# x tiles turned in 32x32 blocks by VectorE, straight into the buffer where they are modulated

## The reference, cut to what matters

```python
def rms_norm(x, g):
    y = xf * lax.rsqrt(jnp.mean(xf * xf, axis=-1, keepdims=True) + EPS)
    return (y * g)
...
    h = rms_norm(x, norm_g) * (1 + scale) + shift
    proj = h @ w_in
```

## Time and profile before

| what | us |
|---|---|
| median of 3 runs (1575.09 to 1575.93) | 1575.82 |
| the profiled execution, its own time | 1577.34 |
| its span in the trace | 1575.4 |
| TensorE busy | 1543.2 (98%) |
| VectorE busy | 793.8 (50%) |
| ScalarE busy | 554.5 (35%) |
| GpSimd busy | 824.7 (52%) |

### The profile page before, as it was taken

The page is one execution under the profiler, slowest core; times in us unless marked ns, Lnnn a source line. Parts: engine busy times, 40 slices in busy tenths (PEclk is TensorE's granted clock), DMA queues, the critical chain, the costliest instruction groups (busy, mean ns, idle before and its releaser), DMA issues.

```text
span 1575.4 us, 31999 instructions
## 1 busy us (share of the span) xinstructions
PE 1543.2 (98%) x13128; PEld 1251.8 (79%) x13128; DVE 793.8 (50%) x1946; ACT 554.5 (35%) x1131; POOL 824.7 (52%) x1080
## 2 busy tenths in 40 slices
PE   5999999999999999999999999999999999999998
PEld 2777788877888778888779877888888977888886
DVE  3677455233468875332344775622355775623132
ACT  4334423434332542333432452244433343243330
POOL 2425424457673553455766372437777363437671
PEclk9899999999999999999999999999999999999999
DMA  9732312344565331233265331224465331223351
GB/s 320 224 84 80 84 54 56 107 122 121 174 176 131 92 93 56 68 110 115 85 187 135 88 108 47 77 68 120 147 185 136 88 108 56 70 67 94 106 161 64
DMA packets 304969, 175.83 MB, mean 112 GB/s; under 512 B 74158, under 2 KB 290567, under 8 KB 304808
## 3 DMA queue, kind: packets, MB, share of 16 engines
q1 hardware_dynamic: 304824, 173.79, 38.4%
HBM read 159.69 MB, written 11.96 MB: 109 GB/s over the span
## 4 chain that ended last, share of the span: by engine, by line
PE 93%; DVE 3%; SPq 2%; DMA 1%; issue 1%; ACT 0%; DVEq 0%
PE ps_D L766 55%; PE ps_D L763 24%; SPq L518 2%; PE ps_XD L826 2%; PE ps_XA L924 1%; PE ps_XB L902 1%; PE ps_XA L955 1%; PE ps_XB L950 1%; PE ps_XB L949 1%; DMA th_t<-in_w_ada 1%; PE ps_XA L902 1%; PE ps_XA L935 1%; PE ps_XC L837 0%; PE ps_XC L942 0%; PE ps_XB L935 0%
## 5 line engine op out<-in xcount | busy, mean ns | idle before, releaser
L1698 POOL TENSOR_TENSOR w_lo_t<-w_raw,w_hi_t 128x256 fp32r<-128x256 f32 x928 | 679.9, 766 | 611.9 <-ACT w_hi_t L981 611.6
L766 PE MATMUL ps_D<-h_hi_t,w_hi_t 128*128 128x512 f32 x1024 | 412.2, 403 | 0.0
L766 PE MATMUL ps_D<-h_hi_t,w_lo_t 128*128 128x512 f32 x1024 | 400.2, 391 | 0.0
L766 PE MATMUL ps_D<-h_lo_t,w_hi_t 128*128 128x512 f32 x1024 | 399.9, 391 | 0.0
L981 ACT ACTIVATE w_hi_t<-w_raw 128x1024 fp32r<-128x1024 f32 x232 | 240.6, 1051 | 83.9 <-DMA w_raw<-in_w_out 35.0
L766 PEld LDWEIGHTS ps_D<-h_hi_t,w_hi_t 128*128 128x128 f32 x1024 | 192.4, 188 | 47.2 <-issue 10.0
L766 PEld LDWEIGHTS ps_D<-h_hi_t,w_lo_t 128*128 128x128 f32 x1024 | 192.2, 188 | 41.6
L766 PEld LDWEIGHTS ps_D<-h_lo_t,w_hi_t 128*128 128x128 f32 x1024 | 192.7, 188 | 36.4
L763 PE MATMUL ps_D<-w_hi_t,h_hi_t 128*128 128x384 f32 (+1 forms) x384 | 141.7, 369 | 1.0 <-DVE yf_t L1338 1.0
L763 PE MATMUL ps_D<-w_hi_t,h_lo_t 128*128 128x384 f32 (+1 forms) x384 | 136.6, 356 | 0.0
L763 PE MATMUL ps_D<-w_lo_t,h_hi_t 128*128 128x384 f32 (+1 forms) x384 | 136.6, 356 | 0.0
(11 more groups left out here) (391 smaller groups left out, 2376.2 us busy)
## 6 DMA issues: line engine op xcount, KB each, us to landing
w_raw<-in_w_in SPq DMA_DIRECT2D x72, 512.0 KB, 4.1
w_raw<-in_w_merge SPq DMA_DIRECT2D x64, 512.0 KB, 3.9
w_raw<-in_w_in SPq DMA_DIRECT2D x64, 256.0 KB, 4.0
w_raw<-in_w_out SPq DMA_DIRECT2D x32, 512.0 KB, 4.2
x_or_AT<-in_x_prompt SPq DMA_DIRECT2D x20, 512.0 KB, 5.1
w_raw<-in_w_proj_a SPq DMA_DIRECT2D x64, 128.0 KB, 2.9
w_raw<-in_w_proj_b SPq DMA_DIRECT2D x32, 256.0 KB, 3.2
xr<-in_x_prompt SPq DMA_DIRECT2D x16, 512.0 KB, 5.5
```

What stands on the lines that cost most here:

```text
L766: ins = mm(bank[:, :], w[:, s0, k0 + k, :], a[:, k, :], start=go, stop=end)
L1698: ins = g_.tensor_tensor(w_lo[:, c, k:k + 2], w_raw[:, n % NRAW, k:k + 2], f32(w_hi[:, c, k:k + 2]), ALU.subtract)
```

## The change

The tiles of passes 1 to 3 come from a second copy of x in DRAM, made on the host (outside the timed program), in which each 32x32 block of a tile is placed so that a blockwise transpose gives the turned tile. A row of such a tile holds, in four groups of 256 columns, pieces of four tokens. So the squares are summed per group (four instructions per tile, 16 columns), a new side task `xs` at unit 50 adds and spreads the parts over the partitions by four small matmuls with `eye32` into XC, and VectorE makes 16 scales from it (`group_scales` in place of `row_scales`). ScalarE scales each tile in four parts. VectorE turns the tile by one transpose of 1024 columns from `x_t` into `hf` (`turn_x`, counted by `x_turned`) and modulates in place (`x_mod`). The turn on TensorE and its use of XA and XB are gone for these tiles. SyncE's loads of tiles 2 and 3 wait for `x_turned`.

```diff
-        put(it, 50, 1, "rstd", 0)
+        put(it, 50, 0, "xs", 0, "XC")
...
-            put(it, (60, 61, 63, 64)[_t], 1, "xT", _t, "XB" if _t % 2 else "XA")
+            put(it, (60, 61, 63, 64)[_t], 1, "xT", _t)
...
-                load(x_t[:, t % 2], x[(it + 1) * TB + P * t:(it + 1) * TB + P * t + P, :], f"x_in{t % 2}")
+                load(x_t[:, t % 2], A["x_blocks"][NT * (it + 1) + t], f"x_in{t % 2}")
...
-                    s.wait_ge("xst", 8 + 8 * it + 4)
+                    s.wait_ge("xst", 8 + 16 * it + 8)
                     x_tile(it, 0), x_tile(it, 1)
                 elif what == "x23":
-                    s.full(it, "xT", a - 2)
+                    s.wait_ge("x_turned", NT * it + a - 1)
                     x_tile(it, a)
...
-                if task == "xT":
-                    x_turn(it, a, x_t[:, a % 2])
-                    return
...
+                elif task == "xs":
+                    s.wait_ge("xst", 8 + 16 * (it + 1))
+                    for g in range(4):
+                        ins = mm(bank[32 * g:32 * g + 32, 0:16], eye32[:, :], xst4, start=True, stop=True)
...
             def scale_x(it, t, src):
                 s.wait_ge("rstd", it + 2)
-                s.done(fn(src, src, ACT.Copy, scale=rst[:, t:t + 1]), "xn")
+                if it < 0:
+                    s.done(fn(src, src, ACT.Copy, scale=rst[:, t:t + 1]), "xn")
+                    return
+                for i in range(4):
+                    part = src[:, 256 * i:256 * i + 256]
+                    ins = fn(part, part, ACT.Copy, scale=rst4[:, 4 * t + i:4 * t + i + 1])
+                s.done(ins, "xn")
+
+            def group_squares(src, t, junk):
+                for i in range(4):
+                    s.wait_ge("xst", s.n.get("xst", 0))
+                    s.done(fn(junk, src[:, 256 * i:256 * i + 256], ACT.Square,
+                              accum_out=xst4[:, 4 * t + i:4 * t + i + 1]), "xst")
...
-                s.freed(it, "xT", t)
+                s.wait_ge("x_mod", NT * it + t + 1)
                 s.done(fn(h_hi[:, :, P * t:P * t + P], hf[t % 2], ACT.Copy), "h_hi")
...
+            def group_scales(it, key):
+                s.full(*key)
+                a, t, u = oss, ow1, ow2
+                free(ts(a, bank_of(key)[:, 0:16], 1.0 / D, EPS, ALU.mult, ALU.add), *key)
+                rsqrt(rst4, a, t, u)
+                do(ts(rst4, rst4, 1.0, None, ALU.mult), "rstd")
...
+            def turn_x(it, t):
+                s.wait_ge("xn", NT * (it + 1) + t + 1)
+                s.wait_ge("h_lo", h_tiles(it, t - 2) if t >= 2 else h_tiles(it - 1, t + 2))
+                do(v.transpose(hf[t % 2].rearrange("p k (a q) -> p a k q", a=4),
+                               x_t[:, t % 2].rearrange("p (a k f) -> p a k f", a=4, k=KT)), "x_turned")
+
             def modulate(it, t):
-                s.full(it, "xT", t)
-                s.wait_ge("h_lo", h_tiles(it, t - 2) if t >= 2 else h_tiles(it - 1, t + 2))
-                bank = pb[BANK[(it, "xT", t)]]
                 for k in range(KT):
-                    ins = ts(hf[t % 2][:, k, :], bank[:, P * k:P * k + P], gscale[:, k, 8:9], shift[:, k, 8:9],
+                    ins = ts(hf[t % 2][:, k, :], hf[t % 2][:, k, :], gscale[:, k, 8:9], shift[:, k, 8:9],
                              ALU.mult, ALU.add)
-                free(ins, it, "xT", t)
+                do(ins, "x_mod")
...
-                elif task == "rstd":
-                    row_scales(it)
+                elif task == "xs":
+                    group_scales(it, key)
                 elif task == "xT":
+                    turn_x(it, a)
                     modulate(it, a)
...
-                                    s.full(it - 1, "xT", 3)
-                                    s.freed(it - 1, "xT", 3)
+                                    s.wait_ge("x_mod", NT * it)
...
+def x_blocks(x):
+    return np.ascontiguousarray(x[0].reshape(SEQ // P, 4, 32, KT, 4, 32).transpose(0, 4, 2, 1, 3, 5)).reshape(SEQ // P, P, D)
```

More of the change, by code:

```diff
@@ L255 @@
         + [f"w_in{n}" for n in range(NRAW)] + ["w_hi", "w_lo", "burst", "th_full", "kk", "sq", "ssq", "qa", "k_sc",
-           "lvl", "dgp", "at0", "smax", "p_exp", "p_norm", "kst", "on", "yf", "yh", "yl", "y7f", "y7h", "y7l", "x_in0", "x_in1", "xst", "rstd",
+           "lvl", "dgp", "at0", "smax", "p_exp", "p_norm", "kst", "on", "yf", "yh", "yl", "y7f", "y7h", "y7l", "x_in0", "x_in1", "xst", "rstd", "x_turned", "x_mod",
            "xn", "h_hi", "h_lo", "grow", "s_rows", "s_th", "s_sq8", "s_sc", "s_exp", "s_p", "ckv", "s_oT",
@@ L420, in build @@
         esel = sb("esel", [P, NS], F32R)
-        sm = sb("sm", [P, 688])
+        sm = sb("sm", [P, 720])
         def small(n, start=[0]):
@@ L432, in build @@
         xst, rst, xw1, xw2, xw3 = small(8), small(4), small(4), small(4), small(4)
+        xst4, rst4 = small(16), small(16)
         bst, mv, rs8, t8, u8 = small(12).rearrange("p (a b) -> p a b", a=2), small(2), small(1), small(1), small(1)
@@ L1142, in side @@
                     s.unit_left(it, "pb", 1)
-                    squares(x_t[:, a % 2], a, R2[:, 512:1024])
+                    group_squares(x_t[:, a % 2], a, R2[:, 512:768])
                 elif task == "sx_":
@@ L1808 @@
     arrays = {n: np.ascontiguousarray(inputs[n]) for n in INS}
+    arrays["x_blocks"] = x_blocks(arrays["x_prompt"])
     arrays.update(constants())
```

## The result

The changed kernel takes 1578.70 us (median of 8 runs, 1576.93 to 1581.43) where the kernel before took 1575.66 beside it (8 runs, 1573.86 to 1577.51). The ratio is 1.0020, with a 95% interval of 1.0011 to 1.0029: slower by 0.2%, 1.7 to 4.6 us. The forecast was 1575.0; the time lies in its range, and on the other side of "no change" than its sum. The profiled execution took 1577.53 us for a span of 1575.5.

A forecast was written before the change was run, and what follows sets the result against it. TensorE, busy 98% of the span, was taken to bound the kernel. Two passes at -1.8 us, +1.4 for the second pass and +1.3 for small matmuls gave -0.9: 1575.0 us, range 1569 to 1583.

The forecast's parts named there:

- Twelve tiles leave TensorE: Three pass changeovers: the transposes leave TensorE, 3.7 us in the first and third pass, 3.5 in the second, 10.9 in all.
- The small matmuls: Unit 50 of each pass: four new small matmuls on TensorE, nothing hiding them, 0.44 us each, 1.3 in all.
- Turn and modulation: VectorE per tile: turn 1.24 us; eight modulations starting 0.25 apart alone, some 0.8 each beside a busy GpSimd.
- First and third pass: Changeovers: TensorE waits 1.0 us for a bank and 0.8 at unit 68, so 1.8 of 3.7 saved per pass.
- Other waits that move: GpSimd's clearing of AT at unit 2, uses of banks XA, XB and XC, and the loads: put at nothing.
- the price of the second pass: Second changeover: last w_out block lands late, burst at unit 62 starts 3.2 us later, pass ends 1.4 later.
- the clock cannot take this back: Changeover stretch: clock at its upper level, 2.4 GHz, throughout, so time from removed transposes is not lost to it.
- It gets 1.76 back by tiles 2 and 3: Second pass after the late burst: TensorE regains 1.76 us of the 3.2 lost, leaving the pass 1.4 later.
- Rival A: Changeovers: VectorE is not late, modulations take 2.1 us per tile and the removal shows; -6.5 us, 1569.3; chance 0.25.
- Rival B: Changeovers: each tile's first modulation is held until GpSimd's whole run ends; +6 us, 1582; chance 0.22.
- Rival C: VectorE's turn is much dearer than the diff says; at twice 1.24 us, +3 to +8, 1580; chance 0.08.

The follow-up runs named there:

- E2: Changed kernel with the loads of the sample states one unit earlier in SyncE's list: 1574.46 us, ratio 0.9996 to the kernel before.
- E6: Kernel before, with x tile 3 of the second pass loaded behind w_out and the sample states one unit earlier: 1574.00 us, ratio 0.9997.
- E7: Kernel before, with SyncE also waiting for VectorE's modulation of tile 1 before loading x tile 3 in the second pass: 1581.10 us, ratio 1.0040.
- E4: Changed kernel with the modulation done by ScalarE in place of VectorE: 1570.34 us, ratio 0.9967 to the kernel before.
- E8: Changed kernel with VectorE's modulation cut to its first instruction of eight, output not the layer's: 1570.32 us, ratio 0.9968 to the kernel before.
- E3: Changed kernel with x tile 3 of the second pass loaded behind w_out and the sample states one unit earlier: 1568.64 us, ratio 0.9962 to the kernel before.
- E9: Changed kernel with each turn of a tile done twice on VectorE: 1585.84 us, ratio 1.0065 to the kernel before.
- E1: Changed kernel with x tile 3 of the second pass loaded one unit later, behind the last w_out block: 1572.27 us, ratio 0.9980 to the kernel before.

## Why the prediction was right or wrong

**Twelve tiles leave TensorE: right.** The shift falls by 3.7 us each in the first and third pass; 3.7 was put down.

**The small matmuls: right.** 0.4 us each, as put down. But "nothing" for the other waits at unit 50 was wrong by 0.37: in the second pass the next user of XC waits for VectorE's scales.

**Turn and modulation: right, a little dear.** The turn was to take 1.24 and takes 1.246, not held by GpSimd. The Trainium skill (SBUF — State Buffer, "Who interferes with whom") says that a VectorE instruction with at most one SBUF input and outside the 2-port modes does not contend with GpSimd; the 3 ns between the shortest and the longest of the 12 turns agree. The modulations were to start 0.25 apart alone and 0.8 beside GpSimd, six of eight beside it in the first tile; they start 0.26 and 0.70 apart, and it is six of eight. GpSimd was to lose 0.1 per turn and loses nothing. The chain in the first pass was to be done with tile 0 at 427.5 and tile 1 at 435.6; with 3.6 us added back, the shift ahead of unit 60, they are done at 426.8 and 434.3. ScalarE's scaling of a tile in four parts takes 1.67 us for 1.09, 0.6 more and not 0.3; no wait comes of it in the first pass's changeover.

**First and third pass: too dear.** The 1.3 us by which tile 1 is earlier let VectorE empty the bank of unit 62 by 435.0 on the same count, ahead of the 435.3 at which TensorE wants it, so the wait of 1.0 at unit 64 does not come; at unit 68 it is 0.6, not 0.8. Saved 3.0 per pass, not 1.8. To this point the change is a gain, 6.1 us in two passes.

**The first failed step is "Other waits that move ... Nothing for these".** The walk of the first pass ended at unit 68. Within two units behind it stand the sample states, whose load is in SyncE's queue behind blocks that wait for GpSimd's last w_lo. The changed chain leaves that issue 3.1 us earlier in the trace and TensorE 6.7, and I asked only who waits for the tiles. It costs 3.8 us in the trace (E2 brings 3.8 back in the medians, 3.3 in its trace).

**The second is the price of the second pass.** The place, the mechanism and the wait were right: the burst was to start 3.2 us later; against the shift before the changeover it starts 2.8 later. What failed is "It gets 1.76 back by tiles 2 and 3: the pass comes out 1.4 us later". I had argued from the upper clock level in the earlier trace rows that "the clock cannot take this back", and then put a hole of 5 us into TensorE's queue without asking the same again. Behind the hole the burst, the transposes and the first dense matmuls run at 1.2 GHz: 1.2 us by unit 63 and 0.3 in it. At unit 64 TensorE waits 0.62 for the samples' gate product, queued on VectorE behind the modulations. From unit 60 to unit 65 the pass costs 3.3, not 1.4.

**A third part was put at nothing and stays open.** "Nothing for these" closed the list of other waits, and it fails at one more place. In the third and the fourth pass the shift grows between units 19 and 26, by 1.1 and 0.7 us in the changed kernel. One piece of it is a gap inside a run of small matmuls, with no releaser named by the profile:

```profile
997.52 0.37 PE L904 MATMUL ps_XA<-qq,kk 128*32 128x16 f32 x19 [0.54 <-issue]
```

The same stretches grow by 1.2 to 1.8 us together in all eight traces of the changed kernel and its variants, and by nothing in E6 and E7, which are the kernel before with an edit. So it comes with the change. It is there in E4 and E8 too, so it is not the modulation on VectorE; what it is was not tried. A step of 0.3 to 0.6 at the same units of the first pass comes and goes in both kernels.

**The sum again**, from the profile: -3.0 -3.1 (two passes) + 3.8 (states) + 3.3 (second pass) + 1.2 (xs) + 0.4 (XC) = +2.6. The pair of profiles shows +4.9; 2.1 of the 2.3 left are the steps just named, 1.8 in the third and fourth pass and 0.3 in the first. The medians' difference is 3.0, with an interval of 1.7 to 4.6. That the forecast missed by only 3.7 us is in part luck: two passes were too dear by 2.4 together, which hid part of what the two failed steps had left out.

**The rivals.** Rival A's gain of 6.5 did not come, and neither did its mechanism: 59 of the 96 modulations were held by GpSimd. That E3 gains 6.0 comes of two loads moved, and bears it out by number only. Rival B, slower, came in sign but not in mechanism: no modulation was caught for a whole run of GpSimd. Rival C's sensitivity was right (E9: +7.1 for the turn at twice its time, +3 to +8 put down), its premise not: the turn takes 1.246 us. (The chances of "slower" add up to 0.27, not 0.28.)

## What to carry to other kernels

When work leaves the bounding engine, that engine arrives early at everything behind: list what each queue holds for the next few units past the edit, loads above all, and ask which of them is still late when the consumer comes 4 us sooner. Put loads that TensorE itself waits for ahead of loads that wait for another engine. Price a hole of 2 us and more in TensorE's queue as the hole and the work at the lower clock level that follows it. And read single instructions, not the mean of a merged row, where two speeds can be mixed in it.

## What the runs showed of the hardware

**The clock behind a hole.** Every hole of 2.1 us and over behind the prologue, eleven of them in the changed kernel, E1, E2, E4, E7, E8 and E9 (2.13 to 5.63 us), had work at the lower level behind it, some 3 us of it, and 5 to 6 in E7 and at the states in E9. The hole at unit 60 of the second pass is in all eleven traces: of 1.69 to 1.94 us in eight, with the level kept, and of 1.95 (E4), 2.13 (E7) and 2.29 us (E9) in three, with a fall. The windows behind it, of the kernel before (hole of 1.87), of E4 and of E7:

```profile
797.20:801.00 3.80, 3.73 (x16) 3.12 (x17) 0.00 (x0) 1.38 (x2) 3.80 (x6) 1.00 1.01 393
```

```profile
790.20:792.20 2.00, 1.98 (x5) 1.63 (x6) 0.00 (x0) 1.32 (x2) 2.00 (x4) 0.54 1.03 410
```

```profile
793.80:795.80 2.00, 1.98 (x5) 1.62 (x6) 0.00 (x0) 0.64 (x2) 2.00 (x4) 0.56 1.00 395
```

With it goes a loss of 1.6 us in E4 that the changed kernel, with a hole of 1.94, does not have. And after E2's hole of 4.34 the burst ran at nearly full speed (1.15 us) and the matmuls behind it at half, where the changed kernel's burst took 1.94: the level falls within the hole or up to 1.6 us after work resumes (at the states of the changed kernel).

**VectorE beside GpSimd.** A modulation of 128 columns in SBUF shows 0.34 us with GpSimd idle (37 of 96) and starts 0.26 after the last; beside GpSimd's subtractions of 0.7 it shows 0.77 in the median (59 of 96) and starts 0.70 after, one for one, and GpSimd is not slowed. In exchange none was held over several of them, as the addition of 5.96 us had been before.
